# Last group of the output projection: products added into the residual by DMAs instead of by VectorE

## The reference

```python
merged = sum(gate[n] * (branches[n] @ w_branch[l, n]) for n in range(N_BRANCH))
y = merged @ w_out[l]                                  # (512, 2048) @ (2048, 2048)
h = layer_norm(alpha * h + y, ln_g[l], ln_b[l])        # over the 2048 columns of each frame
```

## Time and profile before

| | |
|---|---|
| time, median of 3 runs | 1892.21 us (1890.68 to 1892.37) |
| time of the profiled execution | 1891.88 us |
| its span | 1890.3 us |
| TensorE busy | 1852.8 us, 98% of the span |
| VectorE, ScalarE, GpSimd busy | 1218.0, 826.5, 167.7 us |
| bytes moved by DMAs | 271.94 MB, mean 144 GB/s |
| granted TensorE clock, mean | 0.994 |

### The profile page before, as it was taken

How to read it: one execution, slowest core, us unless ns; L and a number is a source line. 1 busy time by engine, 2 the same in 40 slices (tenths; PEclk the granted TensorE clock), 3 DMA queues, 4 the chain that set the end, 5 groups by cost and what they waited for, 6 DMA issues and landing times.

```text
span 1890.3 us, 24314 instructions
## 1 busy us (share of the span) xinstructions
PE 1852.8 (98%) x8599; PEld 1530.0 (81%) x8599; DVE 1218.0 (64%) x1914; ACT 826.5 (44%) x1353; POOL 167.7 (9%) x230
## 2 busy tenths in 40 slices
PE   8999999999999999999989999999999999999995
PEld 6888887888888888888878888888888888887884
DVE  5754335654555554677868878778787655576757
ACT  4652222544444444344445455455456333234543
POOL 1100000000000000000000000000001000003233
PEclk9999999999999999999999999999999999999998
DMA  8554446433333333333241623615437544439996
GB/s 299 194 155 125 123 140 204 117 85 96 102 91 91 93 85 97 98 95 103 85 168 65 212 90 134 223 28 195 154 114 252 203 146 146 154 118 232 241 239 160
DMA packets 226520, 271.94 MB, mean 144 GB/s; under 512 B 12768, under 2 KB 150032, under 8 KB 224272
## 3 DMA queue, kind: packets, MB, share of 16 engines
q1 hardware_dynamic: 195568, 181.95, 31.0%
q0 software_dynamic: 30880, 89.04, 17.1%
HBM read 231.48 MB, written 37.32 MB: 142 GB/s over the span
## 4 chain that ended last, share of the span: by engine, by line
PE 96%; DVE 2%; DMA 1%; ACT 1%; issue 0%; POOL 0%; POOLq 0%; SPq 0%; ACTq 0%; DVEq 0%
PE acc L618 13%; PE acc L620 13%; PE acc L619 13%; PE scores L940 4%; PE scores L942 4%; PE scores L938 4%; PE acc L938 3%; PE acc L940 3%; PE acc L942 3%; PE transposed L645 3%; PE scores L1008 2%; PE scores L1009 2%; PE scores L1010 2%; PE acc L1008 2%; PE acc L1009 2%; PE acc L1010 2%
## 5 line engine op out<-in xcount | busy, mean ns | idle before, releaser
L618 PE MATMUL acc<-h_hi,w_lo 128*128 128x512 f32 x1056 | 420.7, 398 | 0.0
L620 PE MATMUL acc<-h_hi,w_hi 128*128 128x512 f32 x1056 | 412.0, 390 | 0.0
L619 PE MATMUL acc<-h_lo,w_hi 128*128 128x512 f32 x1056 | 411.1, 389 | 0.0
L1521 DVE TENSOR_TENSOR w_lo<-raw_weights,w_hi 128x1024 fp32r<-128x1024 f32 x214 | 260.9, 1222 | 229.0 <-ACT w_hi L1090 223.6
L1090 ACT ACTIVATE w_hi<-raw_weights 128x1024 fp32r<-128x1024 f32 x214 | 225.8, 1058 | 278.2 <-PE acc L620 115.8
L1340 ACT ACTIVATE piece_split<-w 128x512 fp32r<-128x512 f32 x336 | 212.0, 632 | 221.5 <-PE acc L942 81.4
L1968 DVE TENSOR_TENSOR piece_split<-w,piece_split 128x512 fp32r<-128x512 f32 x336 | 231.9, 691 | 87.4 <-ACT piece_split L1340 78.5
L620 PEld LDWEIGHTS acc<-h_hi,w_hi 128*128 128x128 f32 x1056 | 198.2, 188 | 42.5
L618 PEld LDWEIGHTS acc<-h_hi,w_lo 128*128 128x128 f32 x1056 | 198.9, 188 | 41.0 <-issue 2.8
L619 PEld LDWEIGHTS acc<-h_lo,w_hi 128*128 128x128 f32 x1056 | 198.6, 188 | 39.6 <-issue 1.0
L938 PE MATMUL scores<-piece_split,h_sums 128*128 128x512 f32 x216 | 84.0, 389 | 0.0
(11 more groups left out here) (422 smaller groups left out, 3523.0 us busy)
## 6 DMA issues: line engine op xcount, KB each, us to landing
raw_weights<-in_w_in SPq DMA_DIRECT2D x134, 512.0 KB, 3.8
w<-in_w_in SPq DMA_DIRECT2D x96, 512.0 KB, 8.2
raw_weights<-in_w_branch SPq DMA_DIRECT2D x48, 512.0 KB, 5.1
raw_weights<-in_w_mem_kv SPq DMA_DIRECT2D x32, 512.0 KB, 5.8
gate<-gate_scratch POOLq DMA_DIRECT2D x12, 1024.0 KB, 6.7
out_w_x<-in_w_out POOLq DMA_DIRECT2D x16, 512.0 KB, 8.4
gate_scratch<-first_product POOLq DMA_DIRECT2D x12, 512.0 KB, 6.7
x_rows<-in_x SPq DMA_DIRECT2D x4, 1024.0 KB, 9.5
```

What stands on the lines that cost most here:

```text
L618: pe.matmul(bank_out, wl, hi[:, k, :], start=first, stop=False)
L619: pe.matmul(bank_out, wh, lo[:, k, :], start=False, stop=False)
L620: return pe.matmul(bank_out, wh, hi[:, k, :], start=False, stop=last)
L1521: dve.tensor_tensor(w_lo[:, slot, :], raw[:, slot, :], w_hi[:, slot, :].bitcast(F32), ALU.subtract).then_inc(lo_ready, 1)
```

## The change

In group 1 alone:

- ScalarE copies every product but G4 out of PSUM, some with a scale of -1 (`copy_out`): G1 at its place at (G2, 0); G3 to `o_c12` at (G2, 1); G5 to `o_v` at (G6, 0); G2 to `o_s1` at (G6, 3); G6 to `o_c12` at (G7, 3); G7 to `o_v` at (G4, 3). Before it reuses a buffer it waits until the DMA that read it has landed.
- POOL adds the copies into `resid` by eight accumulating DMAs of 512 KB, from on-chip memory to on-chip memory (`add_to_resid`). They stand behind the last sum of weights on its queue, and several wait for an earlier one.
- VectorE adds only G7 to quarter 21 and G4 to quarter 21. Its statistics wait for the landings of the adds.
- SP issues the two loads of the residual and the loads of ln_g and ln_b.
- The last tile is finished by VectorE in two halves, which are stored plainly by SP and by ScalarE's queue.
- The step semaphores of VectorE are merged into one.

```diff
+            sp.wait_ge(pc_mult, OUT_BASE + double(1, G3, 3) + 1)
+            for done in (st_c11, st_c12, st_c21, st_c22):
+                sp.wait_ge(done, 16 * (GROUPS + 1))
+            for h in range(2):
+                if h:
+                    sp.wait_ge(pc_mult, OUT_BASE + double(1, G5, 3) + 1)
+                sp.dma_start(resid[:, 2 * h:2 * h + 2, :], ...).then_inc(resid_loaded[h], 16)
+            sp.wait_ge(o_sum[G4][0], 16 * DOUBLES * OUT_GROUPS)
+            split_done(1, G6, 3)
+            sp.dma_start(g2_row[:, :], ln_g[0].partition_broadcast(P)).then_inc(rows2_loaded, 16)
+            sp.dma_start(b2_row[:, :], ln_b[0].partition_broadcast(P)).then_inc(rows2_loaded, 16)
...
+                    if g and (p, d) == (G2, 1):
+                        act.wait_ge(st_c12, 16 * (GROUPS + 1))
+                        copy_out(G3, x, o_c12, ev_c12, -1.0)
                     if (p, d) == (G6, 0):
                         act.wait_ge(st_c22, 16 * (GROUPS + g))
+                        copy_out(G5, y, o_v, ev_s5, -1.0 if g else 1.0)
+                    if g and (p, d) == (G6, 3):
+                        act.wait_ge(st_c11, 16 * (GROUPS + 2))
+                        copy_out(G2, w, o_s1, ev_c11)
+                    if g and (p, d) == (G7, 3):
+                        act.wait_ge(st_c12, 16 * (GROUPS + 2))
+                        copy_out(G6, z, o_c12, ev_u2, -1.0)
+                    if g and (p, d) == (G4, 3):
+                        act.wait_ge(st_c12, 16 * (GROUPS + 3))
+                        act.wait_ge(st_c22, 16 * (GROUPS + 2))
+                        copy_out(G7, w, o_v, ev_c22, -1.0)
...
+                    if (p, d) == (G7, 2):
+                        dve.wait_ge(st_c11, 16 * (GROUPS + 3))
                         for t in range(2):
                             stats_tile(t, 2)
+                    if (p, d) == (G4, 1):
+                        dve.wait_ge(st_c12, 16 * (GROUPS + 4))
                         for t in range(2):
                             stats_tile(t, 3)
+                            moments(t)
+                    if p == G4 and d >= 2:
+                        centre(d - 2, slice(0, D)).then_inc(centred, 1)
...
+            def add_to_resid(half_t, quarter, buf, done):
+                pool.dma_start(resid[:, 2 * half_t:2 * half_t + 2, quarter * 512:(quarter + 1) * 512], buf[:, :, :],
+                               accum_op=ALU.add).then_inc(done, 16)
+            ev = 2 * (GROUPS + 2)
+            pool.wait_ge(resid_loaded[0], 16)
+            pool.wait_ge(ev_s1, ev)
+            add_to_resid(0, 2, o_s1, st_c11)
+            pool.wait_ge(ev_c12, ev + 2)
+            add_to_resid(0, 3, o_c12, st_c12)
+            pool.wait_ge(ev_s5, ev + 2)
+            pool.wait_ge(resid_loaded[1], 16)
+            add_to_resid(1, 3, o_v, st_c22)
+            pool.wait_ge(st_c12, 16 * (GROUPS + 2))
+            add_to_resid(0, 3, o_v, st_c12)
+            pool.wait_ge(ev_c11, ev)
+            pool.wait_ge(st_c11, 16 * (GROUPS + 2))
+            add_to_resid(0, 2, o_s1, st_c11)
+            pool.wait_ge(ev_u2, ev)
+            pool.wait_ge(st_c12, 16 * (GROUPS + 3))
+            add_to_resid(0, 3, o_c12, st_c12)
+            pool.wait_ge(st_c22, 16 * (GROUPS + 2))
+            add_to_resid(1, 3, o_c12, st_c22)
...
             rstd(0)
             rstd(1)
+            pool.wait_ge(ev_c22, ev)
+            pool.wait_ge(st_c22, 16 * (GROUPS + 3))
+            add_to_resid(1, 3, o_v, st_c22)
             store_tile(0)
```

More of the change, by code:

```diff
@@ L140, in settle @@
     def settle(self):
[L141 removed]
+        self.eng.wait_ge(self.sem, self.i * self.per + self.n + self.base)
     def close(self):
@@ L469, in program @@
         scaled = sem("tile_scaled")
-        last_half = sem("last_half_tile_ready_and_stored")
+        rows2_loaded = sem("ln_rows2_loaded")
+        last_half = sem("last_half_tiles_ready")
+        half_stored = [sem(f"last_half_tile_stored{h}") for h in range(2)]
         preset = sem("out_preset")
         out_stored = sem("out_stored")
-        dve_o = sem("vector_step_out")
         block = ctx.enter_context(nc.Block())
@@ L1810, in _ @@
             job_done(CH_KV + 3)
-            steps = Steps(dve, dve_kv, 4)
+            steps = Steps(dve, dve_once, KV_STEPS, base=LN_STEPS + F_STEPS)
             for g in range(2):
@@ L2239, in _ @@
                         continue
-                    z, x, y, w = out_pairs[1:] + out_pairs[0:1]
                     if (p, d) == (G1, 3):
                         quarter_21()
-                    if (p, d) == (G6, 0):
-                        dve.wait_ge(resid_loaded[0], 16)
-                    if p == G6 and d < 2:
+                    if p == G6:
+                        dve.wait_ge(resid_loaded[d // 2], 16)
                         stats_tile(d, 0)
                         stats_tile(d, 1)
-                    if (p, d) == (G6, 2):
-                        multiplied_through(1, G3)
-                        for t in range(2):
-                            steps.mark(add_rows(t, 3, x[t][:, :], ALU.subtract))
@@ L2275, in _ @@
                         for t in range(2):
                             stats_tile(t, 3)
-                        moments(0)
-                        moments(1)
-                    if p == G4 and d in (1, 2):
-                        centre(d - 1, slice(0, D)).then_inc(centred, 1)
-            for t in range(2):
-                steps.mark(add_rows(2 + t, 3, o_v[:, t, :], ALU.subtract))
-            steps.settle()
-            multiplied_through(1, G7)
-            for t in range(2):
-                steps.mark(add_rows(2 + t, 3, w[t][:, :], ALU.subtract))
+                            moments(t)
@@ L2296, in _ @@
                     multiplied_through(1, G4)
+                steps.settle()
                 steps.mark(add_rows(t, 2, z[t - 2][:, :], ALU.add))
+                if t == 2:
+                    dve.wait_ge(st_c22, 16 * (GROUPS + 4))
+                    for tile in (2, 3):
+                        stats_tile(tile, 3)
                 steps.settle()
@@ L2302, in _ @@
                     centre(t, slice(0, D)).then_inc(centred, 1)
-            centre(3, slice(BW, D)).then_inc(centred, 1)
-            steps.mark(centre(3, slice(0, BW)))
+            halves = slice(0, BW), slice(BW, D)
+            for half in halves:
+                steps.mark(centre(3, half))
             steps.settle()
             dve.wait_ge(rstd_ready, TT + 4)
-            dve.scalar_tensor_tensor(out=resid[:, 3, 0:BW], in0=resid[:, 3, 0:BW], scalar=small[:, 3, 3:4],
-                                     in1=b2_row[:, 0:BW], op0=ALU.mult, op1=ALU.add).then_inc(last_half, 1)
+            for half in halves:
+                z = resid[:, 3, half]
+                dve.scalar_tensor_tensor(out=z, in0=z, scalar=small[:, 3, 3:4], in1=b2_row[:, half],
+                                         op0=ALU.mult, op1=ALU.add).then_inc(last_half, 1)
             steps.close()
@@ L2508, in _ @@
                 for p, d in OUT_SEQ[g]:
-                    if g and (p, d) == (G2, 0):
-                        pool.wait_ge(pc_mult, OUT_BASE + double(g, G3, 3) + 1)
-                        for done in (st_c11, st_c12, st_c21, st_c22):
-                            pool.wait_ge(done, 16 * (GROUPS + 1))
-                        load_resid(0)
                     if p in (G1, G3, G5, G2):
```

104 lines of the change are left out of this document (37 added, 67 removed).

## The result

The changed kernel takes **1901.85 us** (median of 5 runs, 1901.66 to 1903.91), the kernel before beside it 1891.46 (1890.68 to 1892.37): ratio 1.0057, 95% interval 1.0042 to 1.0072. It is 10.4 us slower. The forecast was 1906, 14.5 slower, range 1897 to 1912.

The account below looks back on a forecast made before the run. TensorE, busy 98% of the span, was taken to bound the kernel. TensorE's end 12.8 us later (7.2, 5.1, 0.5) plus a 1.7 longer tail gave +14.5 on 1891.9: 1906.4, stated as 1906, range 1897 to 1912.

Parts of the forecast that it names:

- Off VectorE, onto ScalarE: Some 9 us of additions leave VectorE, mostly beside TensorE; ScalarE's eight more copies cost nothing, their waits do.
- First landing and first pause: First add lands at 1851.6 behind the sums; ScalarE waits before copying G2, so G7 begins late: +7.2 us.
- Second pause: VectorE waits at (G7, 2) for the fifth add until 1865.9, so TensorE waits for (G7, 3)'s low part: +5.1 us.
- rival 2: Clock falls after a pause: half-clock matmuls, up to 3.4 us per pause, hidden after the first; 1909 to 1911, chance 0.16.
- Issue to landing: With idle engines a 512 KB add lands 5.5 us after issue, bounds 5.0 and 6.5.
- G4 (+0.5): Pause of 1.45 us before (G4, 3) stays and becomes about 2: +0.5 us; TensorE ends at 1884.4.
- Tail: After TensorE's end, POOL's roots and the eighth add (landing 1884.6) delay VectorE; last landing 1902.6, tail 1.7 us longer.
- main case: The summed terms hold: 1906, within 1902 to 1910 by bounds of landing and add engine time; chance 0.63.
- rival 1: SP's loads get a smaller share, so G4's sums and first adds land up to 5 us earlier: 1900, chance 0.14.
- 3 and 4: Faster, adds landed before their waiters come: 1887.5, chance 0.04; even, adds cheap as plain transfers: within 0.2%, chance 0.03.
- (c): Sign: adds land 10 us or more after issue in the full queue, 5 to 6.5 in the idle one.
- (d): Sign: SP's two residual loads land by 1825 and 1836.

Follow-up runs that it names:

- e1: The changed kernel, but POOL issues both residual loads at their old places and the statistics needing them come later: 1904.67 us, ratio 1.0069.
- e3: The changed kernel, but each add into the residual moves only 128 of its 512 columns, same instructions and waits: 1894.12 us, ratio 1.0013.
- e8: The changed kernel, but POOL issues the first two adds between the second and third sum for G4: 1902.75 us, ratio 1.0056.
- e6: e5 with the last quarter (22) of tiles 2 and 3 added by two DMAs issued late: 1887.15 us, ratio 0.9979.
- e2: The changed kernel, but SP issues ln_g and ln_b only after the fifth add has landed: 1901.15 us, ratio 1.0051.
- e5: The kernel before with only the last tile's two halves finished on VectorE and stored plainly by SP and ScalarE: 1889.17 us, ratio 0.9987.
- e7: e6 with tile 1's centring moved behind the low part of (G4, 3); measured twice: 1888.12 and 1887.35 us, the second profile being e7_again.
- e9: e7 with tile 2 stored by a plain DMA instead of an adding one, output lacking ln_b there: 1885.04 us, ratio 0.9967.
- e4: The changed kernel, but VectorE adds G1 and G2 into quarter 11 as before and that quarter's two adds fall away: 1900.20 us, ratio 1.0042.

## Why the prediction came out as it did

- **Off VectorE, onto ScalarE.** The nine microseconds taken off VectorE bought nothing, as forecast: VectorE was idle for 10.0 us in one wait instead. ScalarE's copies took 0.58 to 0.60 us each; its wait was the cost.
- **First landing and first pause (+7.2).** In the span of this execution the first add should have landed at 1851.6 - 0.96 = 1850.6; it did at 1850.0. Pause 6.32 us; G7 begins 6.5 us late. Right, 0.7 too large. SP's loads did overtake, but landed at 1827.0 and 1838.3, where 1824 and 1835 were forecast in this frame: the first packets of SP's queue moved 3.5 us behind the issue (1818.0 after 1814.50), not 1.5 as I had it. e1 confirms that the loads' queue is no matter, e3 and e8 that the place behind the sums is.
- **Second pause (+5.1).** The fifth add lands at 1865.5, forecast 1865.9 - 0.96 = 1864.9. That it fits so well is luck: two errors cancel. The packets of ln_g and ln_b, issued at 1847.5, move only from about 1851.5, so the second add lands 1.9 us sooner than forecast (1854.4 against 1856.3). For the same reason ln_g, ln_b and the third add are still in the queue, until 1857.0, 1860.6 and 1860.1, when the fourth and fifth are issued, and these take 8.0 and 9.8 us in place of 5.5 and 6.8. The idle time of TensorE is 3.67 us only, because TensorE arrives 2.8 us late: from 1853.4 to about 1858.6 the granted clock was at half, that is 1.2 of 2.4 GHz, after TensorE had stood for 6.3 us, and matmuls followed one another by 0.43 us in place of 0.23. So rival 2's mechanism did occur, in the harmless place that the prediction gave it ("hidden by the second"). (G7, 3) begins 6.5 us further behind, 1.4 more than the term.
- **Issue to landing.** Unloaded 5.1 us where I took 5.5, and 5.0 to 5.2 in e6 and e2 as well: the low end of my bounds. The rows' arithmetic, 2.6 fixed and 2.5 for the bytes, was exact; e3's 3.2 for a quarter of the bytes fits too (2.6 + 0.6). The estimate of 3.2 us for 512 KB from the Trainium skill's page "DMA: Bandwidth & Descriptors", section on the anatomy of one DMA by the SWDGE path, is 1.9 us below what an add takes with idle engines. It prices bytes at 436 GB/s, near the 424 to 430 of the plain loads in the earlier trace rows, and the accumulating DMAs there move at 207 and 211.
- **G4 (+0.5).** Measured +0.1, by other means: the pause of 1.45 us is gone, and some 1.5 us are lost at half clock instead, in the last double of G7, behind the pause of 3.67 us (matmuls from 1869.1 to 1872.1 follow one another by 0.43). That is rival 2's mechanism once more, here at the place where it counts, but for less than half of the 3.4 us that it was given. TensorE's end was forecast +12.8 and is +13.0. The small errors of three terms cancelled.
- **Tail (+1.7): the term that failed.** It is -2.0. I let the two roots on POOL end at 1879 and the eighth add land at 1884.6, with VectorE waiting. They took this:

```profile
1871.34 0.22 POOL L2567 TENSOR_SCALAR small<-mean_var 128x1 f32<-128x1 f32 x1 [5.42 <-DVE mean_var L2198]
1871.65 0.57 POOL L2570 TENSOR_TENSOR small<-small,minus_half 128x1 f32<-128x1 f32 x1
1872.21 0.95 POOL L2567 TENSOR_SCALAR small<-mean_var 128x1 f32<-128x1 f32 x1
1873.24 2.53 POOL L2570 TENSOR_TENSOR small<-small,minus_half 128x1 f32<-128x1 f32 x1
```

  4.4 us from 1871.3 to 1875.8, not 7.1, and the eighth add landed at 1880.8, 0.1 us after VectorE had come to the statistics. VectorE's last pass, of two halves, then ends at 1893.1:

```profile
1890.61 2.48 DVE L2320 SCALAR_TENSOR_TENSOR resid<-resid,small,ln_b_row 128x1024 f32<-128x1024 f32 x2 [0.92 <-POOL small L2570]
```

  In the frame of this execution the forecast was 1896.0. SP's store of the first half doesn't wait for both passes, as I had it, but goes out at 1892.0, so that 4.0 us were gained up to the issue; 2.1 were given back, as it took 7.7 us to land and not 5.6, in engines that the tiles' stores still filled. ScalarE's store, issued at 1893.1, landed last, at 1899.8 (6.7 us), 1.8 before the forecast. And the span ends 0.5 us behind the last landing, not 2.2 as before, where the last store was POOL's: 1.7 more that no term of mine had. The two make the 3.5 us by which the sum was too high, and the 0.96 of the shift the rest of 4.6 (1906.4 against 1901.84).
- **Rivals.** The time alone doesn't choose between them: 1901.85 is just outside the 1902 to 1910 of the main case and nearer to rival 1's 1900 (whose own terms, 2, 5, 0.5 and 1.7, add up to 9, not 8). The trace does. 1 fell: from 1820 to 1825 the engines took 173 packets of SP's and 168 of POOL's, though a load's packets are four times as large, the last sum for G4 landed at 1847.5, and the first pause was 6.3 us, not 2. 3 and 4 fell, though their gains were real: e5 finds 2.5 us of them. What a quarter of the bytes leaves, 1894.1, is still no gain over e5: even cheap adds don't pay where a low part stands behind them.

**Signs named beforehand.** (a) ScalarE's wait was 10.5 us, not 12, and ended at 1850.0. (b) VectorE's wait came, to 1865.6, but the pause was 3.67 and not 5. (c) came in the main: 10.9 to 19.6 us in the full queue for the first three adds, but 8.0 and 9.8 for the fourth and fifth, and 5.1 in the idle one. (d) didn't: the loads landed 3 us late. (e), the wait for the eighth add, did not come. Of the signs of being wrong none did: the clock was below 1.0 in G7, and back at 1.0 when G4 began.

The half clock belongs to the pauses: in the kernel before, e5, e6, both of e7, and e9, whose longest pause here is 1.53 us, the granted clock reads 1.00 from 1800 to the last matmul. Below 1, and down to 0.50, it is behind the pauses of 3.61 to 11.78 us in the change, e1 to e4 and e8, as it was behind the stop of 2.71 us in the earlier trace rows.

What stays open: the 0.96 us by which group 1 ran early, and which of two conditions makes an add dear. e6's adds have both idle engines and nobody waiting; no run leaves the adds in the full queue with the waits moved behind the low parts.

## What to carry to other kernels

Work moved from an engine with slack to DMAs is not free when the DMA queue is full: read the share in the windows and the landing times at the places where the moved work would stand, and count what is queued behind its waiter. The same add costs nothing where the engines are idle and nobody waits (e6), and 8 to 20 us of latency where they aren't. Before removing a pause of the busiest engine, look whether the tail is bound by something else (e7, e9): then it only gets to wait elsewhere.

## What the runs showed that I had not expected

- An adding DMA of 512 KB between two on-chip buffers takes the same 2.5 us of all engines as the sums that read HBM: in e2 the second and third adds, issued 0.7 us apart, land after 12.7 and 14.5 us, so 2.5 apart, and the fourth and fifth after 5.3 and 7.2, so 2.6 apart.
- POOL's operations on 128x1 values take 0.22 to 2.5 us for the same form (TENSOR_TENSOR 0.57 and 2.53 above). It is not noise: the roots of tiles 0 and 1 take 0.22, 0.57, 0.95 and 2.53 in the change, e1, e3, e4 and e8 alike, and 1.10, 2.52, 0.79 and 2.53 before and in e5. What sets them these traces don't tell, so that a changed program can move such a sum by 2 to 3 us.
- ln_g and ln_b, 1 MB each and landing 9.5 and 12.8 us after SP's issue, moved a pause of TensorE by their place alone (e2): a load that nobody waits for yet is still a delay for what is in flight beside it.
- A half tile stored plainly lands 4.9 us (e2) to 8.6 us (e7_again) after issue; the one run that changes only the stores in flight ahead of it (e9) moves it from 8.4 to 6.0.
- SP's packets start late while POOL's queue is full: in the change, after the issues at 1814.50, 1825.39 and 1847.46, the first ones moved 3.5 to 4 us later, in e4 3.5 and in e8 4.2. In e1 and e3 it was 1.4 us, and these traces don't tell what makes the difference.
